# Two attention/state-space layers: the SSM decay tiles, the convolution's first tap and the order of the SSM steps

## The reference

```python
def hybrid_layer(x, w_in, conv_w, conv_b, dt_bias, a_log, ...):
    proj = jnp.einsum("bld,de->ble", x, w_in)
    q, k, v, z_attn, z_ssm, xbc, dt_raw = jnp.split(proj, IN_SPLITS, axis=-1)
    attn = sliding_window_attention(q, k, v, sinks) * jax.nn.silu(z_attn)
    xbc = jax.nn.silu(causal_depthwise_conv(xbc, conv_w, conv_b))      # 4 taps, 1536 channels
    xs, bm, cm = jnp.split(xbc, ...)
    dt = jax.nn.softplus(dt_raw + dt_bias)
    y = ssd_chunked(xs, dt, -jnp.exp(a_log), bm, cm) + xs * d_skip
    ssm = gated_rmsnorm(y, z_ssm, ssm_norm_w)
    out = jnp.einsum("ble,ed->bld", jnp.concatenate([attn, ssm], axis=-1), w_out)
    return layer_norm(DEEPNORM_ALPHA * x + out, ln_g, ln_b)

# in ssd_chunked, chunks of 128 tokens, 16 heads of 64, 2 groups:
    a_cs = cumsum(dt * a)                                  # per head, over the chunk
    y_diag = einsum(cb, exp(a_cs[l] - a_cs[s]) for s <= l, xdt)
```

## Time and profile before

| | |
|---|---|
| runs | 2075.69, 2080.3, 2088.3 us |
| median | 2080.3 us |
| profiled execution: its own time, its span | 2075.69 us, 2074.0 us |
| mean granted TensorE clock | 0.909 of full speed |
| HBM traffic over the span | 266 GB/s |

### The profile page before, as it was taken

One profiled execution on the slowest core, in us unless ns is written; L12 is line 12 of the kernel. 1 busy time (PEld: TensorE's weight loads), 2 busy tenths in 40 slices (PEclk: granted clock), 3 DMA queues, 4 the chain that ended last, 5 costly groups with the idle time before them and its releaser, 6 DMA issues.

```text
span 2074.0 us, 21120 instructions
## 1 busy us (share of the span) xinstructions
PE 1695.1 (82%) x9180; PEld 1031.2 (50%) x9180; DVE 563.0 (27%) x1306; ACT 294.3 (14%) x783; POOL 11.5 (1%) x35
## 2 busy tenths in 40 slices
PE   8999999999999999866566766656667575899888
PEld 6675477645488886532123323321223231468754
DVE  0473414633341412411111111111011110116552
ACT  0243303422112100100100000000000001112220
POOL 0000000000000000000000000000000000000000
PEclk9999999999999999897888878888788888999989
DMA  9442263348253374699999999999999999544100
GB/s 348 140 99 76 83 222 122 122 130 276 89 203 122 125 270 160 270 428 427 428 428 428 427 427 428 427 427 427 427 428 427 427 428 394 195 162 163 41 1 21
DMA packets 106614, 553.35 MB, mean 267 GB/s; under 512 B 7856, under 2 KB 10416, under 8 KB 82960
## 3 DMA queue, kind: packets, MB, share of 16 engines
q1 hardware_dynamic: 105664, 548.81, 66.9%
q0 software_dynamic: 848, 3.05, 0.4%
HBM read 550.79 MB, written 1.05 MB: 266 GB/s over the span
## 4 chain that ended last, share of the span: by engine, by line
PE 66%; DMA 24%; DVE 6%; ACT 3%; issue 1%; SPq 0%; DVEq 0%; ACTq 0%
PE bank L629 34%; DMA ring<-in_w 13%; DMA arena<-in_w 10%; PE bank L1084 7%; PE bank L1057 6%; PE bank L638 5%; PE bank L1105 5%; PE bank L617 2%; ACT arena L1456 1%; PE bank L846 1%; DVE arena L1951 1%; PE bank L675 1%; PE bank L780 1%; PE bank L760 0%; DMA ring<-in_w_in 0%
## 5 line engine op out<-in xcount | busy, mean ns | idle before, releaser
L629 PE MATMUL bank<-arena,ring 128*128 128x256 f32 x1856 | 413.8, 381 | 2.7 <-DVE arena L2768 2.2
L1084 PE MATMUL bank<-ring,arena 128*32 128x512 f32 x1216 | 283.5, 728 | 152.9 <-DMA ring<-in_w 98.9
L629 PE MATMUL bank<-ring,arena 128*128 128x512 f32 (+5 forms) x1000 | 381.2, 536 | 15.2 <-ACT arena L1380 3.0
L629 PEld LDWEIGHTS bank<-arena,ring 128*128 128x128 f32 x1856 | 350.8, 191 | 54.2 <-issue 7.2
L1084 PE MATMUL bank<-arena 128*32 128x512 f32 x832 | 232.9, 724 | 97.5 <-DMA ring<-in_w 51.8
L629 PEld LDWEIGHTS bank<-ring,arena 128*128 128x128 f32 x1000 | 186.9, 198 | 181.6 <-issue 150.9
L1084 PEld LDWEIGHTS bank<-ring,arena 128*32 128x32 f32 x1216 | 72.0, 131 | 283.4 <-issue 283.4
L1057 PE MATMUL bank<-arena 128*128 128x128 f32 x512 | 126.4, 421 | 29.7 <-DVE arena L2480 28.6
L1057 PEld LDWEIGHTS bank<-arena 128*128 128x128 f32 x512 | 123.4, 335 | 43.4 <-DVE arena L2480 41.3
L1084 PEld LDWEIGHTS bank<-arena 128*32 128x32 f32 x832 | 58.2, 130 | 174.0 <-issue 173.8
L1105 PE MATMUL bank<-ring,arena 128*32 128x512 f32 x608 | 109.6, 594 | 6.8 <-ACT arena L1666 6.8
(11 more groups left out here) (368 smaller groups left out, 1220.0 us busy)
## 6 DMA issues: line engine op xcount, KB each, us to landing
ring<-in_w SPq DMA_DIRECT2D x114, 2048.0 KB, 31.1
arena<-in_w SPq DMA_DIRECT2D x78, 2048.0 KB, 30.8
ring<-in_w_in SPq DMA_DIRECT2D x42, 2048.0 KB, 8.1
ring<-in_w_out SPq DMA_DIRECT2D x6, 2048.0 KB, 7.9
ring<-in_w_ada SPq DMA_DIRECT2D x6, 2048.0 KB, 8.1
ring<-in_w_out SPq DMA_DIRECT2D x16, 512.0 KB, 9.2
ring<-in_w_conv_out SPq DMA_DIRECT2D x2, 2048.0 KB, 8.5
ring<-in_w_attn_out SPq DMA_DIRECT2D x2, 2048.0 KB, 7.8
```

What stands on the lines that cost most here:

```text
L629: i = te.matmul(ps, lhsT, rhs, start=n0 + k == 0, stop=n0 + k == n - 1)
L1084: m = te.matmul(ps[32 * j:32 * j + 32, :], LM.xg[:, f, 128 * k + 32 * j:128 * k + 32 * j + 32], vs[j][:, 512 * (k % 2):512 * (k % 2) + 512 ...
```

## The change

1. `layer_order`: the rule for the SSM steps. Now s0 stands behind p34 and then one step behind each p, never two; what is left comes in a row at the end. Up to s8 (behind p42) only s0 moves. Then in layer 0: p43 s9 p44 s10 p45 s11 p46 s12 p47 s13 p48 s14 p49 s15 s16 s17 s18 s19. In layer 1 the same up to p49 s15, then p50 s16 p51 s17 p52 s18 s19.
2. The "mb" tiles: four products (broadcast column of `adt`) x `tri`, which give the cumulative sum along the columns directly, instead of four transposes of `acs`.
3. The subtraction of the decay tile goes from ACT (relu, four instructions) to DVE (`tensor_scalar` with subtract and min, four instructions), in the same step as DVE's product with CB. ACT's exp waits for it.
4. The convolution's tap 0 goes from ACT to DVE, and tanh and the last multiply of a tile are issued in the tile's own step, not one step late.

```diff
@@ layer_order
-    att_on = False
+    att_on = ssm_on = False
...
-        for _ in range(1 if done == 20 else 0 if done < 36 else 2 if ns in (8, 11, 13, 16) else 1):
-            if ns < 20:
-                out.append("ssm")
-                ns += 1
+        if ssm_on and ns < 20:
+            out.append("ssm")
+            ns += 1
...
+        if i == 34:
+            ssm_on = True
@@ tensor_program, layer_ssm
-                            t.wait_ge(*at.of("ev", "acs", ly))
-                            turn(("mb", ly, tt, g, q),
-                                 [(128 * i, bc(L1.acs[:, tt, 8 * g + 4 * q + i:8 * g + 4 * q + i + 1], 128)) for i in range(4)])
+                            ps = fresh("mb", ly, tt, g, q)
+                            for i in range(4):
+                                hd = 8 * g + 4 * q + i
+                                m = te.matmul(ps[:, 128 * i:128 * i + 128], bc(L1.adt[:, tt, hd:hd + 1], 128), tri[:, :],
+                                              start=True, stop=True)
+                            m.then_inc(*t.done("mm", "mb", ly, tt, g, q))
@@ scalar_program, layer_proj
-                def conv_tanh(ch):
+                for ch in CONV:
+                    ready(("mm", "cv", ly, ch), ("zpad", ly))
+                    se.mul(L1.xb[:, ch, 3:259], bank("cv", ly, ch)[:, 0:256], 0.5).then_inc(*a.done("ev", "cv", ly, ch))
                     to = scratch(("cv", ly, ch), 256)
                     a.wait_ge(*at.of("conv", ly, ch))
                     se.activation(to, L1.cv[:, ch, :], ACT.Tanh).then_inc(*a.done("tanh", "cv", ly, ch))
-                for n, ch in enumerate(CONV):
-                    ready(("mm", "cv", ly, ch), ("zpad", ly), ("cb", ly))
-                    se.mul(L1.xb[:, ch, 3:259], bank("cv", ly, ch)[:, 0:256], 0.5).then_inc(*a.done("ev", "cv", ly, ch))
-                    a.wait_ge(*a.last())
-                    se.activation(L1.cv[:, ch, :], L1.xb[:, ch, 0:256], ACT.Identity, scale=prm[:, C_W + ch:C_W + ch + 1],
-                                  bias=prm[:, C_B + ch:C_B + ch + 1]).then_inc(*a.done("tap", ly, ch))
-                    if n:
-                        conv_tanh(CONV[n - 1])
                     yield
...
-                        if g + tt == 0:
-                            conv_tanh(CONV[-1])
@@ scalar_program, layer_ssm
-                            last = ("mm", "yb", ly, tt, g - 1) if g else ("mm", "yb", ly, 0, 1) if tt else ("mm", "st", ly, 1)
-                            ready(("mm", "mb", ly, tt, g, q), last)
-                            for i in range(4):
-                                hd = 8 * g + 4 * q + i
-                                m = se.activation(L1.Mt[:, 4 * q + i, :], bank("mb", ly, tt, g, q)[:, 128 * i:128 * i + 128],
-                                                  ACT.Relu, scale=-1.0, bias=L1.acs[:, tt, hd:hd + 1])
-                            m.then_inc(*a.done("ev", "mb", ly, tt, g, q))
-                            a.wait_ge(*a.last())
+                            a.wait_ge(*at.of("Mdiff", ly, tt, g, q))
                             mv = L1.Mt[:, 4 * q:4 * q + 4, :]
-                            se.activation(mv, mv, ACT.Exp, scale=-1.0).then_inc(*a.done("Mexp", ly, tt, g, q))
+                            se.activation(mv, mv, ACT.Exp).then_inc(*a.done("Mexp", ly, tt, g, q))
@@ vector_program, layer_proj
-                def conv_gated(ch):
+                for ch in CONV:
+                    ready(("ev", "cv", ly, ch), ("cb", ly))
+                    ve.tensor_scalar(L1.cv[:, ch, :], L1.xb[:, ch, 0:256], prm[:, C_W + ch:C_W + ch + 1],
+                                     prm[:, C_B + ch:C_B + ch + 1], ALU.mult, ALU.add).then_inc(*v.step())
+                    for k in range(1, 4):
+                        behind()
+                        ve.scalar_tensor_tensor(...)
+                    v.also("conv", ly, ch)
                     v.wait_ge(*at.of("tanh", "cv", ly, ch))
                     ve.scalar_tensor_tensor(L1.cv[:, ch, :], tmp[...], 1.0, L1.cv[:, ch, :], ALU.add, ALU.mult
                                             ).then_inc(*v.done("cv", ly, ch))
...
-                for n, ch in enumerate(CONV):
-                    v.wait_ge(*at.of("tap", ly, ch))
-                    for k in range(1, 4):
...
-                    if n:
-                        conv_gated(CONV[n - 1])
@@ vector_program, layer_ssm
+                            last = ("mm", "yb", ly, tt, g - 1) if g else ("mm", "yb", ly, 0, 1) if tt else ("mm", "st", ly, 1)
+                            ready(("mm", "mb", ly, tt, g, q), last)
+                            for i in range(4):
+                                hd = 8 * g + 4 * q + i
+                                m = ve.tensor_scalar(L1.Mt[:, 4 * q + i, :], bank("mb", ly, tt, g, q)[:, 128 * i:128 * i + 128],
+                                                     L1.acs[:, tt, hd:hd + 1], 0.0, ALU.subtract, ALU.min)
+                            m.then_inc(*v.done("ev", "mb", ly, tt, g, q))
+                            v.also("Mdiff", ly, tt, g, q)
                             v.wait_ge(*at.of("Mexp", ly, tt, g, q))
```

More of the change, by code:

```diff
@@ L1940, in layer_proj @@
                     yield
-                def conv_gated(ch):
+                for ch in CONV:
[4 more added lines that the diff above has]
+                        behind()
+                        ve.scalar_tensor_tensor(L1.cv[:, ch, :], L1.xb[:, ch, k:k + 256],
+                                                prm[:, C_W + 12 * k + ch:C_W + 12 * k + ch + 1], L1.cv[:, ch, :],
+                                                ALU.mult, ALU.add).then_inc(*v.step())
+                    v.also("conv", ly, ch)
                     v.wait_ge(*at.of("tanh", "cv", ly, ch))
@@ L1959, in layer_proj @@
                     for tt in range(2):
-                        if g + tt == 0:
-                            conv_gated(CONV[-1])
                         yield
```

## The result

The changed kernel takes 2110.7 us (median of 4 runs, 2108.3 to 2121.3) against 2078.6 us (median of 4 runs of the kernel before), so by the medians it is 32 us slower. The ratio on record is 1.0163, with a 95% interval of 1.0138 to 1.0187, which would be 34 us; the median of all 17 executions of the changed kernel on record is 2114.0 us. The forecast was 2109 us, range 2093 to 2124.

A forecast was written before the change was run, and what follows sets the result against it. PE was taken as the bound (66% of the span's chain, DMA 24%); products 8.0, convolution 9.3, softplus 0, subtraction and order 8.2 and clock 3.4 sum to 28.9 us, on the median 2109 us, range 2093 to 2124.

The forecast's parts named there:

- Products: SSM mb tiles: products cost 0.50 us more a group than transposes, 16 groups, nothing hides it: +8.0 us.
- The broadcast row of the third block: Profile row pricing mb products: eight with a broadcast column take 1.89 us, so four 0.945 against 0.44 for transposes.
- Convolution: Convolution stage: the `pT` copies come later behind tiles in series, so PE waits longer: +9.3 us in two layers.
- The walk: Layer 0's convolution followed tile by tile through ACT's and DVE's queues: PE goes on 2.8, later 5.15 us late, net +4.65.
- Softplus: s0, 27 instructions over 6.1 us, moved behind DVE's last convolution tile: covered by 1.2 us, so 0.
- Subtraction and order: SSM: new PE waits of 2.8 and 5.5 us in layer 0, 2.8 in layer 1, less waits removed: +8.2 us.
- Clock: PE's clock: one more fall in layer 0's convolution and one near its end, about 1.7 us each: +3.4 us.
- a window full of these transposes: Profile window at granted clock 1.00, read as showing no need of products instead of mb transposes to hold the clock.
- Rival B: PE's clock falls at each new idle time, six falls: 10.2 us instead of 3.4, 2116 us; chance 0.15.
- Rival A: Convolution stage: the waits don't appear since PE runs ahead: 17.9 us slower, 2098 us; chance 0.20.
- C: Convolution and end of layer 0: relieving ACT is worth more than the waits: 3 us slower, 2083 us; chance 0.05.
- the stage that DMA bounds: Experts, whose first loads wait for buffers PE frees: the layers' loss arrives in full; absorbing it would prove the prediction wrong.

The follow-up runs named there:

- conv: Kernel before with only the two convolution edits (tap 0 on DVE, tanh and last multiply in the tile's own step): ratio 1.0065, +13.5 us.
- own_step_only: Kernel before with only tanh and last multiply in the tile's own step, tap 0 still on ACT: ratio 1.0091, +19 us.
- tap_only: Kernel before with only tap 0 moved to DVE, tanh and last multiply still one step late: ratio 0.998, -4 us.
- order: Kernel before with only the new `layer_order`, subtraction still on ACT and mb tiles still transposes: ratio 1.0065, +13.6 us.

## Why the prediction was right

The total was right, and for the reasons given in the main: 28.9 us forecast, 32 measured in the medians and 34.0 between the two traces ahead of the experts. That 2109 lies within 2 us of the measured median is in part luck: the forecast stood on a median of 2080.3 of three runs, which a fourth lowered to 2078.6, and all 17 executions on record give 2114.0. By terms:

- **Products.** Forecast +8.0 (0.50 a group), measured 0.45 a group, 7.2 us in the trace and 7.5 alone. The broadcast row of the third block was the right one to take, still a little high.
- **Convolution.** Forecast +9.3 of waits, with one fall of the clock 11.0; alone it costs 13.5. The walk named the instructions at which PE would stand: the first `pT` copy (forecast 4.4 us of waiting and PE going on at 116.4, measured 4.5 and 116.77) and the later one (2.9, measured 3.1). Undersized were the `tensor_scalar` (0.33 taken, 0.41 measured) and, from it, the second round: PE waited 1.5 us for the normalization, and 0.6 for the first one. The waits grew by 5.7 us a layer, not by 4.65. Which of the two edits does it was not separated in the prediction; the runs show that it is tanh in its own step, while the tap is harmless.
- **Softplus.** Forecast 0, measured 0 (1.0002).
- **Subtraction and order.** Forecast idle times of 2.8 and 5.5 us at the end of layer 0, of 2.8 in layer 1, and the waits of 1.5 and 1.2 us gone. The trace has 8.1 in two (longest 5.5) and 2.7, and the two are gone. The waits grew by 8.1 net, so the sum of 8.2 was right, its reason in part wrong: the prediction put the wait of 5.5 us down to DVE's subtraction behind y. The order alone has the same wait, since ACT's square of y blocks its queue in the same way.
- **Clock.** The term that was mis-sized: 3.4 us taken for two falls, about 7.6 left in the trace when waits and products are taken off. The price of a fall, 1.7, is that of 5.14 against the 3.46 us of the same product in layer 0; the 3.67 that the prediction sets beside it is another product. The falls came where the forecast had them, behind the first wait of the convolution in layer 0 and at its end, but also behind the last wait of layer 1 (a yb of 3.65 us), and at the end of layer 0 the slow stretch held yb and yo (5.46 us instead of 2.64), which is more than the 1.7 us of the one row that the price was taken from. In layer 1's modulation, on the other hand, less was lost than before. The prediction also takes "a window full of these transposes" at a clock of 1.00 as a sign that they do not lower it; that window holds 40 of them, 5.95 of PE's 44.99 busy us, among products, so it says little. Rival B, a fall at each new wait, was nearer in size (10.2 us), but of its six new falls three came: none behind the waits of 3.1 us, and next to none behind the first yb wait of layer 0 (yb 2.00 us, yo 0.93).

Rival A (the waits don't appear) and C (relieving ACT is worth more) fall with conv and own_step_only. C has a grain of truth: tap_only is 0.2% faster, though by the clock more than by its waits. Nothing was absorbed by the stage that DMA bounds.

## What to carry to other kernels

With in-order engines, ask of each wait that an edit adds or moves what stands behind it in that queue and who wants it, and walk the few microseconds in which that happens; the totals of load said nothing here, as moving a tap to the busier engine was free and moving two other instructions of the tile by one step cost 0.9%. An engine's order need not be that of the engine it serves: letting the work that nobody waits for lag by one step, on the two serving engines only, took away nearly all waits of the convolution, and together with a better covered end of layer 0 it beat the kernel before by 0.8%. And where PE waits, count the clock's fall behind the wait with the wait itself, as a chance and not as a certainty: one trace of each kernel can't tell a cost from a fall that happened to come.

## What the runs showed of the hardware

Three things were not expected. The clock's fall costs more than half as much again as the waits ahead of it: the order's idle time net of what it removed is some 8 us (5.5 in layer 0, 2.7 in layer 1), its loss 13.6, of which the rows at the end of layer 0 show 5.2 as slower products; keeping PE busy with useless products in those waits gave back 3 us of that in the trace (by the ratios 6, roughly). And a fall can hit several groups in a row: yb twice, with its yo, at 3.06 and 3.64 us instead of 1.73. Last, whether a fall comes behind a given wait is not fixed by its length: behind the same wait of 1.9 us it came in nine of twelve stages of six kernels, at 1.7 us each; behind the 2.7 us at the end of layer 1 it came in the changed kernel (yb 3.65 us) and not in order (1.97); and behind 3.1 us in the changed kernel not at all.
